# Three modulation vectors formed by weighted sums on VectorE instead of split-weight products on TensorE

## The reference

```python
sc = jax.nn.silu(c)
scc = jax.nn.silu(c_ctx)
shift1, scale1, gate1, shift2, scale2, gate2 = jnp.split(sc @ w_mod[l] + b_mod[l], 6, axis=-1)
n_cmod = 2 if last else 6
cmods = jnp.split(scc @ w_mod[l][:, :n_cmod * D_MODEL] + b_mod[l][:n_cmod * D_MODEL], n_cmod, axis=-1)
h = modulate(rms_norm(x, norm1_g[l]), shift1, scale1)
hc = modulate(rms_norm(xc, norm1_g[l]), cmods[0], cmods[1])
y, yc = token_mixer(h, hc, P, last)
x = x + gate1[:, None, :] * y
h = modulate(rms_norm(x, norm2_g[l]), shift2, scale2)
x = x + gate2[:, None, :] * grouped_moe(h, router_w, router_b, moe_w_gate[l], moe_w_up[l], moe_w_down[l])
```

## Time and profile before

| | us |
|---|---|
| median of 3 runs | 1716.15 |
| lowest, highest | 1713.44, 1717.37 |
| span of the profiled execution | 1715.6 |

### The profile page before, as it was taken

The page is one execution under the profiler, slowest core; times in us unless marked ns, Lnnn a source line. Parts: engine busy times, 40 slices in busy tenths (PEclk is TensorE's granted clock), DMA queues, the critical chain, the costliest instruction groups (busy, mean ns, idle before and its releaser), DMA issues.

```text
span 1715.6 us, 22943 instructions
## 1 busy us (share of the span) xinstructions
PE 1621.8 (95%) x9736; PEld 1383.8 (81%) x9736; DVE 1085.0 (63%) x1320; ACT 854.4 (50%) x1012; POOL 8.2 (0%) x18
## 2 busy tenths in 40 slices
PE   7999999999998999999989978899999998899997
PEld 3787868899986777889888856799987976799986
DVE  4677563545656688985466557665566666765555
ACT  5554543544535677764344356454443446344533
POOL 0000000000000000000000000000000000000000
PEclk9899999999999999999999989999999999899999
DMA  7636302236645799995545222455544423455540
GB/s 235 230 128 213 120 17 78 74 99 200 212 157 208 284 330 353 362 371 203 169 148 170 91 74 99 154 190 196 182 168 166 150 97 112 158 196 174 171 172 25
DMA packets 132301, 297.49 MB, mean 173 GB/s; under 512 B 5175, under 2 KB 16744, under 8 KB 131240
## 3 DMA queue, kind: packets, MB, share of 16 engines
q1 hardware_dynamic: 130336, 287.94, 48.7%
q0 software_dynamic: 1104, 5.52, 1.0%
q10 hardware_dynamic: 760, 2.58, 0.4%
HBM read 294.97 MB, written 1.05 MB: 173 GB/s over the span
## 4 chain that ended last, share of the span: by engine, by line
PE 80%; DVE 11%; ACT 6%; issue 1%; DMA 1%; ACTq 0%; DVEq 0%
PE bank L444 79%; DVE cut L1490 4%; ACT cut L2486 3%; PE bank L457 1%; DVE stat L1714 1%; ACT arena L2683 1%; ACT pairs L2492 1%; DVE stat L2313 0%; DVE XT L2333 0%; DVE XT L2327 0%; DVE XT L2310 0%; DMA arena<-in_hy 0%; DMA raw<-in_w_in 0%; ACT arena L2692 0%; DVE pairs L1498 0%
## 5 line engine op out<-in xcount | busy, mean ns | idle before, releaser
L1490 DVE TENSOR_TENSOR cut<-raw,cut 128x2048 fp32r<-128x2048 f32 (+1 forms) x266 | 601.4, 2275 | 354.9 <-ACT cut L2486 354.1
L444 PE MATMUL bank<-pairs,cut 128*128 128x256 f32 (+1 forms) x5480 | 688.7, 286 | 19.2 <-DVE cut L1490 8.8
L444 PEld LDWEIGHTS bank<-pairs,cut 128*128 128x128 f32 (+1 forms) x5480 | 675.3, 191 | 31.0 <-issue 17.9
L2486 ACT ACTIVATE cut<-raw 128x2048 fp32r<-128x2048 f32 (+1 forms) x266 | 502.5, 1899 | 277.3 <-PE bank L444 262.8
L444 PE MATMUL bank<-cut,pairs 128*128 128x512 f32 (+1 forms) x2460 | 590.8, 399 | 21.8 <-DVE cut L1490 18.7
L444 PEld LDWEIGHTS bank<-cut,pairs 128*128 128x128 f32 x2460 | 460.1, 191 | 138.1 <-DVE cut L1490 23.4
L444 PE MATMUL bank<-arena 128*128 128x128 f32 (+10 forms) x748 | 176.6, 392 | 18.1 <-ACT arena L2519 7.1
L444 PEld LDWEIGHTS bank<-arena 128*128 128x128 f32 (+4 forms) x748 | 106.4, 188 | 67.0 <-issue 37.9
L2492 ACT ACTIVATE pairs<-arena 128x256 fp32r<-128x256 f32 (+1 forms) x81 | 37.4, 496 | 80.9 <-DVE arena L2391 51.4
L1498 DVE TENSOR_TENSOR pairs<-arena,pairs 128x256 fp32r<-128x256 f32 (+1 forms) x81 | 40.0, 527 | 31.7 <-ACT pairs L2492 31.6
L2683 ACT ACTIVATE arena<-bank,stat 128x256 f32<-128x256 f32 (+1 forms) x64 | 33.2, 527 | 40.1 <-DVE stat L1716 39.8
(11 more groups left out here) (294 smaller groups left out, 882.3 us busy)
## 6 DMA issues: line engine op xcount, KB each, us to landing
raw<-in_moe_w_gate SPq DMA_DIRECT2D x32, 1024.0 KB, 7.4
raw<-in_moe_w_up SPq DMA_DIRECT2D x32, 1024.0 KB, 7.2
raw<-in_moe_w_down SPq DMA_DIRECT2D x32, 1024.0 KB, 7.1
raw<-in_w_in SPq DMA_DIRECT2D x30, 1024.0 KB, 5.1
raw<-in_w_mod SPq DMA_DIRECT2D x24, 1024.0 KB, 5.2
raw<-in_ffn_w_gate SPq DMA_DIRECT2D x22, 1024.0 KB, 5.1
raw<-in_ffn_w_up SPq DMA_DIRECT2D x22, 1024.0 KB, 5.1
raw<-in_ffn_w_down SPq DMA_DIRECT2D x22, 1024.0 KB, 5.0
```

Source lines behind the costliest of these rows:

```text
L444: return pe.matmul(o, l, r, start=start, stop=stop, skip_group_check=True)
L1490: v.tensor_tensor(both[:, PIECE:PIECE + n], M.raw[K.place(i)[0]][:, 0:n], both[:, 0:n].bitcast(F32), ALU.subtract).then_inc(*up("lo_w", i))
L2486: a.activation(M.cut[K.slot(i)][:, 0:n], M.raw[K.place(i)[0]][:, 0:n], ACT.Copy).then_inc(*up("hi_w", i))
```

## The change

The three vectors 2, 3 and 4 (chunks 4 to 9) are formed in another way. Their `w_mod` pieces are 2 x 128 rows by 1024 columns, four for each vector, loaded but not cut. VectorE multiplies each of the two row blocks by the partition's value of silu(c) and adds it into `mrow`, 128 x 1024 (`partial_sums`). For vectors 3 and 4 TensorE then sums over the partitions with eight matmuls of one column (`mod_vector`), for vector 2 with two of 512 columns against the matrix of ones (`gate_row`). The bias of vector 2 comes in through row 0 of `mrow`: GpSimd clears `mrow` and loads the bias there. The number of bytes loaded is the same; the pieces stand at other places of the stream and count in the levels as others do.

```diff
+        if sums:
+            K.used[i] = ("msum", *sums)
+            return None
...
-        if c not in (4, 5, 10, 11):
-            late.append(c)
+        late.append(c)
+    def mod_sums(v, k0):
+        take(D["w_mod"], k0, 2, 1024 * v, 1024, True, sums=(v, k0))
+    def mod_vector(v):
+        P.wait_ge(*at("mod", 0))
+        P.wait_ge(*at("msum", v, 6))
+        for m in range(8):
+            c = 2 * (8 * v + m)
+            last = mm(bank[0][:, c:c + 1], M.mrow[:, 128 * m:128 * m + 128], C("ones")[:, 0:1], True, True)
+        last.then_inc(*up("modvec", v))
+    def gate_row(c, among):
+        o = claim(("gr", c), ("G", c), among)
+        P.wait_ge(*at("msum", 2, 6))
+        x = 512 * (c % 2)
+        mm(o[:, :], C("ones"), M.mrow[:, x:x + 512], True, True).then_inc(*up("gr", c))
...
-    mod_chunk(6)
+    mod_sums(3, 0)
     convolved(0, 0)
+    mod_sums(3, 2)
     convolved(0, 2)
-    mod_chunk(7)
+    mod_sums(3, 4)
     transposed(1)
-    mod_chunk(8)
+    mod_sums(3, 6)
     spectrum(1)
     queries(0, nothing, nothing)
+    mod_vector(3)
...
     query_spread(2)
-    mod_chunk(9)
...
+    mod_sums(4, 0)
     project("gk", W, 512, 2, (HL, HR), 8, lambda m: ("GKT", m))
+    mod_sums(4, 2)
     project("ga", W, 1184, 1, (HL, HR), 8, lambda m: ("GA", m))
+    mod_sums(4, 4)
     token_major("gv", W, 768, 512, tokens, 8, lambda i: ("GV", i))
+    mod_sums(4, 6)
...
+    mod_vector(4)
     in_chunks(0)
...
     for t0 in range(8, 24, 4):
+        mod_sums(2, t0 // 2 - 4)
         branch_gates(t0, [lambda: None, lambda: None])
-        if t0 < 16:
-            mod_chunk(2 + t0 // 4)
...
     for c in (4, 5):
-        spread_row(c, Q)
+        gate_row(c, Q)
...
+    def partial_sums(i, vec, k0):
+        w(*K.landed(i))
+        x = M.raw[K.place(i)[0]][:, :].rearrange("p (k n) -> p k n", k=2)
...
+            if k0 + k == 0 and vec == 3:
+                w(*at("modcol", 3)[:2])
+                v.tensor_scalar(M.mrow[:, :], x[:, k, :], col, None, ALU.mult).then_inc(*up(*done))
...
+                v.scalar_tensor_tensor(out=M.mrow[:, :], in0=x[:, k, :], scalar=col, in1=M.mrow[:, :], op0=ALU.mult,
+                                       op1=ALU.add).then_inc(*up(*done))
...
+    w(*at("modvec", 4))
+    g.memset(M.mrow[:, :], 0.0).then_inc(*up("mrow0"))
+    w(*at("mrow0"))
+    g.dma_start(M.mrow[0:1, :], D["b_rows"][0:1, :]).then_inc(*up("ld_brow", 0, by=16))
```

More of the change, by code:

```diff
@@ L15 @@
 AX = mybir.AxisListType
-Piece = namedtuple("Piece", "src k0 nk c0 n raw place")
+Piece = namedtuple("Piece", "src k0 nk c0 n raw place sums")
 Held = namedtuple("Held", "hi lo n")
@@ L466, in claim, with take @@
         return bank[b]
-    def take(src, k0, nk, c0, n, raw=False, place=None):
+    def take(src, k0, nk, c0, n, raw=False, place=None, sums=None):
         i = taken[0]
@@ L472, in take @@
         if not K.final and i == len(K.stream):
-            K.stream.append(Piece(src, k0, nk, c0, n, raw, place))
+            K.stream.append(Piece(src, k0, nk, c0, n, raw, place, sums))
+        if sums:
+            K.used[i] = ("msum", *sums)
+            return None
         if raw:
@@ L552, in mod_columns @@
             P.wait_ge(*at("mrow", c))
-            if c >= 4:
-                P.wait_ge(*at("mod", 0))
             for m in range(4):
@@ L997, in tensor_program @@
     for t0 in range(8, 24, 4):
+        mod_sums(2, t0 // 2 - 4)
         branch_gates(t0, [lambda: None, lambda: None])
-        if t0 < 16:
-            mod_chunk(2 + t0 // 4)
     project("gl", D["w_br_gla"], 0, 8, (M.YG,), 4, lambda m: ("tm", 1, m))
     project("at", D["w_br_att"], 0, 8, (M.YA,), 8, lambda m: ("tm", 2, m))
-    mod_columns()
     router_shift()
     for c in (4, 5):
-        spread_row(c, Q)
+        gate_row(c, Q)
     BLOCKS, HALVES = [(0, 0), (0, 1), (1, 0), (1, 1)], [(0, 0), (1, 0), (0, 1), (1, 1)]
@@ L1486, in cut_until @@
             p = K.stream[i]
+            if p.sums:
+                partial_sums(i, *p.sums)
             if not p.raw:
@@ L1491, in cut_until @@
                                 ALU.subtract).then_inc(*up("lo_w", i))
+    def partial_sums(i, vec, k0):
+        w(*K.landed(i))
+        x = M.raw[K.place(i)[0]][:, :].rearrange("p (k n) -> p k n", k=2)
+        if k0 == 0 and vec == 2:
+            w(*K.load("brow", 1))
+        for k in range(2):
+            col = M.sc[:, k0 + k, 0:1]
+            done = ("msum", vec, k0) if k else ("v",)
+            if k0 + k == 0 and vec == 3:
+                w(*at("modcol", 3)[:2])
+                v.tensor_scalar(M.mrow[:, :], x[:, k, :], col, None, ALU.mult).then_inc(*up(*done))
+            elif k0 + k == 0 and vec == 4:
+                w(*at("modvec", 3)[:2])
+                v.tensor_scalar(M.mrow[:, :], x[:, k, :], col, None, ALU.mult).then_inc(*up(*done))
+            else:
+                if k:
+                    w(*at("v")[:2])
+                elif k0:
+                    w(*at("msum", vec, k0 - 2)[:2])
+                v.scalar_tensor_tensor(out=M.mrow[:, :], in0=x[:, k, :], scalar=col, in1=M.mrow[:, :], op0=ALU.mult,
+                                       op1=ALU.add).then_inc(*up(*done))
     P.ahead, P.pieces = cut_until, lambda: n_cut[0]
@@ L1855, in router_factors @@
     def router_factors():
-        w(*at("modcol", 9))
-        v.tensor_tensor(M.mod[:, 24:40, :], M.bank[0][:, 48:80].rearrange("p (m c) -> p m c", c=2),
-                        long(M.vcol("b_mod", 24, 16), 2), ALU.add).then_inc(*up("mod", 1))
+        w(*at("modvec", 4))
+        v.tensor_tensor(M.mod[:, 24:40, 0], M.bank[0][:, 48:80:2], M.vcol("b_mod", 24, 16), ALU.add).then_inc(*up("mod", 1))
         w(*at("mod", 1))
@@ L2621, in scalar_program @@
     input_columns(1)
-    mod_row(6, 2)
-    mod_row(7, 3)
     transposed(1)
-    mod_row(8, 6)
     spectrum(1)
@@ L2664, in scalar_program @@
         norm_copy("ak", h, M.RNa[h], M.RQa[h], K.bank("pj", "ak", h))
-    mod_row(9, 7)
     for h in range(2):
@@ L2771, in scalar_program @@
         branch_gate(m, M.BG[:, m:m + 2, :])
-        if m in (10, 14):
-            mod_row(4 + m // 12, 8 + m // 12)
     for j in range(4):
@@ L3153, in gpsimd_program @@
     at, up, D, w = K.at, P.up, M.D, P.wait_ge
-    g.dma_start(M.mrow[4:5, :], D["b_rows"][0:1, :]).then_inc(*up("ld_brow", 0, by=16))
     w(*at("YA", "a", 15))
     g.dma_start(M.W2[64:128, :], D["w2z"]).then_inc(*up("ld_w2z", by=16))
+    w(*at("modvec", 4))
+    g.memset(M.mrow[:, :], 0.0).then_inc(*up("mrow0"))
+    w(*at("mrow0"))
+    g.dma_start(M.mrow[0:1, :], D["b_rows"][0:1, :]).then_inc(*up("ld_brow", 0, by=16))
     w(*at("YGLA", 1))
```

## The result

The changed kernel takes **1710.12 us** (median, 1705.95 to 1713.86) beside 1716.15 for the kernel before: ratio 0.9967, 95% interval 0.9957 to 0.9978. A second series gave 1711.62 beside 1714.69, ratio 0.9976, 0.9966 to 0.9986. The forecast was 1704 us with a range of 1699 to 1710. The kernel got faster as forecast, but by 3 to 6 us where 12.2 were expected.

What follows compares the result with a forecast made beforehand. The prediction took TensorE to bound the kernel, busy 1621.8 of 1715.6 us. Its terms, -1.3 - 5.2 + 2.0 + 1.8 - 9.5 = -12.2 us, took 1716.15 to 1704 us, range 1699 to 1710.

Steps and rivals of the forecast that it cites:

- 96 products to `convolved(1)`: Hyena stretch: 15.4 us leave TensorE, but waiting for VectorE and a slower clock leave a gain of 1.3 us.
- to the value piece: Before attention: chunk 9 and the columns of chunk 8 go, and all of it is gained, -5.2 us.
- Removed and added work: TensorE, all changed places: 30.6 us of chunks and waits removed, 3.6 us of one-column products added.
- The price of a sum: VectorE: one weighted sum over 1024 columns was estimated at 1.29 us, a piece at 2.6.
- lower bound of 0.75: VectorE's weighted sum: 0.75 us if priced like a product with a scalar alone, giving 1700.2 us in all.
- VectorE's chain in the Hyena stretch: Hyena stretch: VectorE ends `gated(0)` at 138.2, so TensorE stands still over 9 us before `transposed(1)`.
- GLA stretch: Before the GLA queries: a cut at a later place makes TensorE 2.0 us later, bounds 0 and 3.1.
- Branch gates: Branch gates: two groups of 5.0 us go, a late first cut costs 0.5 us, together -9.5 us.
- Rivals 3 and 4: Branch gates: 3, cuts bind, 1708 to 1712, chance 0.12; 4, raw buffers can't keep up, chance 0.03.
- the term for the clock: Behind the standstill before `transposed(1)`: about 4 us at half speed cost 2.0 us, 0 if the clock stays up.
- 3.5 if it takes 7 us to return: Same standstill: upper value of the clock's cost, 3.5 us, if the clock needs 7 us to return.

Runs made afterwards that it cites:

- sums3_filled: Changed kernel with vector 3's sums taken later and 9 idle products before `transposed(1)`: 1701.39 us (0.9915), again 1703.51 us (0.9935).
- fill_hole: Changed kernel with 20 idle products between `convolved(0)` and `transposed(1)`: 1709.17 us, ratio 0.9961.
- both_filled: both_moved with 9 idle products added before `transposed(1)`: 1707.65 us, ratio 0.9951.
- both_moved: Changed kernel with vector 3's sums taken later and vector 4's last piece moved ahead of gv: 1710.57 us, ratio 0.9967.
- chunks2: Changed kernel with vector 2 put back to `mod_chunk`, vectors 3 and 4 still by sums: 1719.12 us, ratio 1.0019.
- not_counted: sums3_filled with summed pieces no longer counted in the lookahead: 1705.82 us beside 1714.16 for the kernel before.
- before_hole: Kernel before with 20 idle memsets on VectorE before the second half of `gated(0)`: 1727.9 us, ratio 1.0073.
- only2: Kernel before with vector 2 alone changed to sums: 1708.14 us, ratio 0.9960.

## Why the forecast missed

Step by step, the two first traces against the terms of the sum (start to start, TensorE):

| place | before | after | difference | of it loss | forecast |
|---|---|---|---|---|---|
| 96 products to `convolved(1)` | 53.54 | 53.47 | -0.1 | +3.2 | -1.3 (2.0 for the clock) |
| to the value piece (207.15, 202.32) | 43.60 | 39.76 | -3.8 | +1.7 | -5.2 |
| attention | 61.91 | 61.98 | +0.1 | 0 | 0 |
| gk to the GLA queries | 45.77 | 47.63 | +1.9 | 0 | +2.0 |
| to the first branch group (349.07, 349.19) | 34.24 | 37.26 | +3.0 | +1.8 | +1.8 |
| to the third group (401.27, 403.39) | 52.20 | 54.20 | +2.0 | +1.5 | +0.5 |
| to the gate rows | 90.53 | 80.40 | -10.1 | 0 | -10.0 |

- **Removed and added work:** right. Net -15.2, or -14.1 counted between starts, against -14.2 (the sum without its 2.0 for the clock). One-column groups 1.84 us, as taken from the earlier trace rows.
- **The price of a sum:** right, 1283 ns for an estimated 1.29 us. The lower bound of 0.75 is out, and the rule of the Trainium skill (VectorE: DVE Perf Modes, "Mode 2x_2P — use both read ports for one tensor") stands: two tensor sources, no double rate.
- **VectorE's chain in the Hyena stretch:** right. Forecast 138.2 in a trace whose stretch began at 110.01; measured 137.51 with a start at 109.09.
- **GLA stretch:** right, 1.79 us for 2.0, from a cut at a new place. Its root is that the lookahead counts summed pieces: with the other counting the wait was 0.20.
- **Branch gates:** right, 0.33 us of wait for 0.5. Rivals 3 and 4 had no sign in the trace: the next wait stands outside the 672 products of the row at 403.39.
- **What failed is the term for the clock.** The forecast gave 2.0 us to one place, from the windows at 74 to 80 us. At that place 3.2 to 3.5 us were lost. And it priced the clock nowhere else: three smaller stretches at 172, 312 and 350 us, of 1.7 us (once 3.4), were in both traces of the changed kernel, more came and went. Together it is 9.2 us where 2.0 stood. The kernel before had next to none between 110 and 490 us, where its TensorE was never idle for more than 2.1 us; the chunks' 512-column products were also what kept the clock up. Taking them out cost twice at the hole: the engine stands, and then it runs slowly. The forecast left this step out of its range too, with "3.5 if it takes 7 us to return" as the only upper bound. The trace of before could have told it: beyond rows 7 it has 16 more stretches of half clock, two of them behind waits of only 1.89 us (796.27) and 1.94 us (877.61), with 1.6 and 1.7 us lost.
- The section "What's actually happening" of the Trainium skill's page TensorE: Matmul & The Clock Gate calls the ramp penalty less than 1% of a typical kernel span; it says so of a kernel's start. The forecast weighed it for a fall in the middle, and would by it have left the clock out. For all falls together that doesn't fit here: the losses are 38.0 and 41.5 us of the kernel before (2.2 and 2.4%), 49.6 and 48.7 after (2.9 and 2.8%).
- **Open:** why nearly the same instructions lose 24.5 to 37.2 us behind 490 us, from kernel to kernel and run to run. For single places no run here tells when the clock falls in a gap of about 2 us and when not.

## What to carry to other kernels

Work taken from the bounding engine is worth its time only where something else is ready; where a chain on another engine ends just behind it (2.1 us of slack here), keep the work or defer that engine's new share past its late step, as sums3_filled does (ratios 0.9915 and 0.9935, ahead of the changed kernel's 0.9967 and 0.9976). Price every new TensorE gap with the granted clock behind it, count half-clock time in both traces before looking for another cause, and compare stretches net of it. A lookahead that is counted in pieces must not count pieces that the cutting engine doesn't handle.

## What the runs showed of the hardware

- Idle products into an unread bank kept the clock at 1.00 behind the hole that they filled (fill_hole, both_filled, sums3_filled). The medians fell with them by 2.4 us (20 products) and 2.9 us (9 of them, both_filled beside both_moved), both with overlapping intervals.
- A hole of 4.1 us was enough for a fall to 0.50, and `spectrum(1)` then took 8.9 to 10.1 us for 7.13.
- The loss behind a long hole varies: 3.2 and 3.5 us behind 9.43, 2.7 behind 9.44 (chunks2), 1.7 behind 9.58 (not_counted), 2.7 behind 11.24 (before_hole).
- The clock also fell where TensorE didn't stand: in both traces of before to 0.50 at about 42 us, in or right behind 16 one-column products (39.31 to 43.20 us in the first, no wait), with 3.4 us lost.
- Behind the same 2.1 us wait at about 172 us the clock fell in one trace of the kernel before and stayed up in the other.
- Runs of one kernel spread by up to 15 us with their mean clock (only2: 1703.46 at 0.978, 1718.24 at 0.969).
